# Where an expert's overflow blocks run in a one-core mixture-of-experts layer on Trainium2

## The reference, cut to what matters

```
top_logit, top_e = lax.top_k(logits, 4);  top_w = softmax(top_logit)
for every expert e, on the tokens routed to it:
    gu   = xb @ w_gu[e] + b_gu[e]                # 1024 -> 2048
    gate = min(gu[:, :1024], 7);  up = clip(gu[:, 1024:], -7, 7)
    act  = gate * sigmoid(1.702 * gate) * (up + 1)
    y    = act @ w_dn[e] + b_dn[e]               # 1024 -> 1024
    out[token] += y * w
```

## Time and profile before

| | |
|---|---|
| median of 3 runs | 1241.69 us (1239.27 to 1242.06) |
| the profiled execution's own time | 1241.96 us |
| its span on the core | 1240.2 us |
| TensorE matmuls busy | 1101.1 us, 89% |
| TensorE weight loads busy | 474.5 us, 38% |
| VectorE busy | 266.9 us, 22% |
| ScalarE busy | 146.2 us, 12% |
| GpSimd busy | 30.1 us, 2% |
| moved by DMA | 426.32 MB, mean 344 GB/s |
| SP's queue | 84.8% of 16 engines' span |
| mean granted TensorE clock | 0.966 |

### The profile page before, as it was taken

One profiled execution on the slowest core, in us unless ns is written; L12 is line 12 of the kernel. 1 busy time (PEld: TensorE's weight loads), 2 busy tenths in 40 slices (PEclk: granted clock), 3 DMA queues, 4 the chain that ended last, 5 costly groups with the idle time before them and its releaser, 6 DMA issues.

```text
span 1240.2 us, 14598 instructions
## 1 busy us (share of the span) xinstructions
PE 1101.1 (89%) x5388; PEld 474.5 (38%) x5389; DVE 266.9 (22%) x767; ACT 146.2 (12%) x309; POOL 30.1 (2%) x53
## 2 busy tenths in 40 slices
PE   7999796998899998989898878999989898989883
PEld 6677445333234332323232332433333232323221
DVE  2354535111112111121111111111211111111113
ACT  2144311100001000001000001001000010100000
POOL 3000410000000000000000000000000000000000
PEclk9999896998899999999999998999999999999997
DMA  9400849730999999999999958999999999999993
GB/s 314 181 1 1 262 191 393 294 137 17 419 419 418 419 418 418 418 417 417 418 419 418 418 232 326 418 417 418 417 418 418 418 418 418 419 418 418 417 414 120
DMA packets 80435, 426.32 MB, mean 344 GB/s; under 512 B 6025, under 2 KB 7610, under 8 KB 47610
## 3 DMA queue, kind: packets, MB, share of 16 engines
q1 hardware_dynamic: 79834, 425.37, 84.8%
q10 hardware_dynamic: 576, 0.61, 0.2%
HBM read 424.91 MB, written 1.05 MB: 343 GB/s over the span
## 4 chain that ended last, share of the span: by engine, by line
PE 50%; DMA 29%; SPq 14%; DVE 3%; issue 2%; ACT 1%; POOL 0%; DVEq 0%; POOLq 0%; ACTq 0%
PE PB L716 48%; DMA WB<-in_w_gate_up_dram 22%; SPq L331 6%; DMA WB<-in_w_down_dram 6%; SPq L326 6%; PE PB L1048 0%; DMA X<-in_x_dram 0%; SPq L335 0%; DVE S L1395 0%; PE PB L723 0%; DVE S L1524 0%; POOL K L478 0%; DVE WB L1289 0%; PE PB L806 0%; DVE S L1504 0%
## 5 line engine op out<-in xcount | busy, mean ns | idle before, releaser
L716 PE MATMUL PB<-WB,S 128*64 128x512 f32 (+5 forms) x3472 | 775.0, 596 | 72.3 <-DMA WB<-in_w_gate_up_dram 62.6
L716 PEld LDWEIGHTS PB<-WB,S 128*64 128x64 f32 (+2 forms) x3472 | 250.0, 140 | 562.8 <-issue 410.5
L1498 DVE TENSOR_SCALAR S<-PB 128x512 f32<-128x512 f32 (+1 forms) x34 | 23.5, 692 | 604.8 <-PE PB L716 604.8
L716 PE MATMUL PB<-S 32*64 32x512 f32 (+5 forms) x464 | 113.7, 594 | 4.9 <-issue 2.5
L659 ACT ACTIVATE S<-S 128x512 f32<-128x512 f32 x32 | 20.2, 630 | 556.4 <-DVE S L1498 556.4
L716 PE MATMUL PB<-S,X 128*128 128x128 f32 (+1 forms) x576 | 75.7, 293 | 9.3 <-DVE S L1524 8.0
L716 PEld LDWEIGHTS PB<-S,X 128*128 128x128 f32 x576 | 72.4, 208 | 23.7 <-issue 21.9
L716 PEld LDWEIGHTS PB<-S 32*64 32x64 f32 (+4 forms) x464 | 41.6, 164 | 65.0 <-issue 58.0
L1542 DVE COPY S<-PB 64x512 f32<-64x512 f32 x32 | 21.9, 683 | 205.4 <-PE PB L716 205.4
L716 PE MATMUL PB<-S,WB 128*128 128x256 f32 (+2 forms) x336 | 63.7, 391 | 0.4 <-ACT S L498 0.4
L716 PEld LDWEIGHTS PB<-S,WB 128*128 128x128 f32 (+1 forms) x336 | 49.5, 178 | 12.5 <-issue 2.1
(11 more groups left out here) (199 smaller groups left out, 339.4 us busy)
## 6 DMA issues: line engine op xcount, KB each, us to landing
WB<-in_w_gate_up_dram SPq DMA_DIRECT2D x128, 2048.0 KB, 22.8
WB<-in_w_down_dram SPq DMA_DIRECT2D x128, 1024.0 KB, 23.0
WB<-in_w_in_dram SPq DMA_DIRECT2D x1, 3088.0 KB, 15.2
WB<-in_w_in_dram SPq DMA_DIRECT2D x1, 3072.0 KB, 20.3
WB<-in_w_in_dram SPq DMA_DIRECT2D x1, 2144.0 KB, 11.1
WB<-in_w_in_dram SPq DMA_DIRECT2D x1, 2048.0 KB, 16.1
WB<-in_w_out_dram SPq DMA_DIRECT2D x2, 1024.0 KB, 10.2
WB<-in_w_out_dram SPq DMA_DIRECT2D x1, 2048.0 KB, 16.7
```

The lines of the kernel that those rows point to most:

```text
L716: return mm_(o, l, r, start=start, stop=stop, skip_group_check=True)
L1498: ts(g, gate, LIMIT, None, ALU.min).then_inc(s[g_ok], 1)
```

## The change

Each expert's extra blocks run at the end of its own gate-up's step, in front of the next expert's gate-up, instead of behind its down. For odd E they now stand right behind the transposes of E's activations in part 1 of the loop, and for even E behind `combine` in part 2. Expert 0's stand ahead of the loop; the number of calls stays 32, of which one is ahead of the loop, 30 are in it and one is behind it (before: none, 30 and two). Since the expert's down has not run yet, the extra block's down waits for each chunk of the down weights itself. The extra gather goes into bank 4 instead of 6; the extra gate-up waits until bank 6 has been copied out (`actT` or `ct_sb`); the wait for the down output copies stands before the transposes, not before the gather. VectorE makes the next expert's bias rows (`next_expert_rows`) ahead of the output copy instead of behind it. SP's program is not changed.

```diff
@@ scalar: extra_slots, and the order
-                act.activation(yx[:, 0:KT * XSLOTS], PB[6][:, 0:KT * XSLOTS], ACT.Copy).then_inc(s["xxg"], 1)
+                act.activation(yx[:, 0:KT * XSLOTS], PB[4][:, 0:KT * XSLOTS], ACT.Copy).then_inc(s["xxg"], 1)
...
             combine_weights(1)
+            extra_blocks(0)
             with act.Fori(0, PAIRS - 1) as i:
                 sigmoid(2 * i + 2)
                 slots_to_sbuf(0, 6, 2 * i + 3)
                 slots_to_sbuf(1, 4, 2 * i + 4)
                 expert_output(0, 2 * i + 1)
-                extra_blocks(2 * i)
                 act_columns(6, 2 * i + 2)
+                extra_blocks(2 * i + 1)
                 sigmoid(2 * i + 3)
                 expert_output(1, 2 * i + 2)
-                extra_blocks(2 * i + 1)
                 act_columns(5, 2 * i + 3)
                 combine_weights(i + 2)
+                extra_blocks(2 * i + 2)
             sigmoid(N_EXPERTS)
             expert_output(0, N_EXPERTS - 1)
-            extra_blocks(N_EXPERTS - 2)
             act_columns(6, N_EXPERTS)
+            extra_blocks(N_EXPERTS - 1)
             expert_output(1, N_EXPERTS)
-            extra_blocks(N_EXPERTS - 1)
@@ tensor: the extra block
-            def extra_gather(outputs_copied):
+            def extra_gather():
...
-                pe.wait_ge(s["ysb_ok"], outputs_copied + 1)
-                pe.wait_ge(s["ysb_dv"], outputs_copied)
                 pe.wait_ge(s["xoh"], xc)
...
-                        ins = mm(PB[6][:, XSLOTS * k:XSLOTS * k + XSLOTS], x_sb[:, b, P * k:P * k + P], ohx[:, b, :],
+                        ins = mm(PB[4][:, XSLOTS * k:XSLOTS * k + XSLOTS], x_sb[:, b, P * k:P * k + P], ohx[:, b, :],
...
-            def extra_blocks(e, t, n):
+            def extra_blocks(e, loaded, t, pb6_copied, copies, outputs_copied):
...
-                        extra_gather(n)
+                        extra_gather()
+                        pe.wait_ge(s[pb6_copied], copies)
                         for c in range(GU_CHUNKS):
                             extra_gate_up_chunk(c, e).then_inc(s["xguc"], 1)
                         extra_gate_up_bias(e).then_inc(s["xgu"], 1)
+
+                        pe.wait_ge(s["ysb_ok"], outputs_copied + 1)
+                        if not (isinstance(outputs_copied, int) and outputs_copied == 0):
+                            pe.wait_ge(s["ysb_dv"], outputs_copied)
                         extra_act_transposes()
...
                         for c in range(DN_CHUNKS):
+                            pe.wait_ge(s_dnl[e][c], 16 * loaded)
                             extra_down_chunk(c).then_inc(s["xdnc"], 1)
@@ tensor: the order
             combine()
+            extra_blocks(0, 1, 0, "ct_sb", 1, 0)
...
                 pe.wait_ge(s["xg_ok"], 2 * i + 4)
-                extra_blocks(0, 2 * i, 2 * i + 1)
                 act_transposes(6, 2 * i + 2)
+                extra_blocks(1, i + 1, 2 * i + 1, "actT", 2 * i + 2, 2 * i + 1)

                 gate_up(0, i + 2, 2 * i + 3)
                 down(1, i + 1, 2 * i + 2)
-                extra_blocks(1, 2 * i + 1, 2 * i + 2)
                 act_transposes(5, 2 * i + 3)
                 weight_transposes()
...
                 combine()
+                extra_blocks(0, i + 2, 2 * i + 2, "ct_sb", i + 2, 2 * i + 2)
...
             down(0, PAIRS, N_EXPERTS - 1)
-            extra_blocks(0, N_EXPERTS - 2, N_EXPERTS - 1)
             act_transposes(6, N_EXPERTS)
+            extra_blocks(1, PAIRS, N_EXPERTS - 1, "actT", N_EXPERTS, N_EXPERTS - 1)
             down(1, PAIRS, N_EXPERTS)
-            extra_blocks(1, N_EXPERTS - 1, N_EXPERTS)
@@ vector: the order in the loop (ahead of and behind it as on the other engines)
                 expert_activations(2 * i + 2)
+                next_expert_rows(0, 2 * i + 1)
                 expert_output(0, 2 * i + 1)
-                extra_blocks(2 * i, 2 * i + 2)
-                next_expert_rows(0, 2 * i + 1)
+                extra_blocks(2 * i + 1, 2 * i + 2)
                 expert_activations(2 * i + 3)
+                next_expert_rows(1, 2 * i + 2)
                 expert_output(1, 2 * i + 2)
-                extra_blocks(2 * i + 1, 2 * i + 3)
-                next_expert_rows(1, 2 * i + 2)
+                extra_blocks(2 * i + 2, 2 * i + 3)
                 next_one_hots(i + 1)
```

More of the change, by code:

```diff
@@ L1568, in _ @@
             expert_activations(1)
+            extra_blocks(0, 1)
             next_one_hots(0)
@@ L1581, in _ @@
             expert_output(0, N_EXPERTS - 1)
-            extra_blocks(N_EXPERTS - 2, N_EXPERTS)
+            extra_blocks(N_EXPERTS - 1, N_EXPERTS)
             expert_output(1, N_EXPERTS)
-            extra_blocks(N_EXPERTS - 1, N_EXPERTS)
             dve.wait_ge(s["comb"], PAIRS + 1)
```

## The result

The changed kernel takes 1225.22 us in the median of 4 runs (1222.96 to 1227.19), against 1240.48 us for the kernel before on the same chip: a ratio of 0.9876, with a 95% interval of 0.9852 to 0.9901. So it is faster by 12 to 20 us, 1.0% to 1.6%; the forecast was 1223.7 us.

What follows compares the result with a forecast made beforehand. Weight DMA was taken as the limit, so only its pauses could shrink: 11.4 (gap 2) + 4.8 (gap 1) + 1.8 (tail) = 18.0 us off 1241.96 gives 1224.0, forecast 1223.7 us; 8-in-10 range 1219 to 1229.

Steps and rivals of the forecast that it cites:

- What bounds the kernel: Weight loads at 418 GB/s set the time and TensorE follows; the change gains only from the DMA's pauses.
- Gap 2: DMA pause of 20.5 us from 730.5 us, around expert 15's extra block; the change was to gain 11.4 us.
- Gap 1: DMA pause of 32.3 us from 276.5 us, around expert 1's extra block; the change was to gain 4.8 us.
- The two skips: First jumps over unused extra-block bodies, ahead of the loop and at its end: 0.5 and 2.5 us, together taken as 2.7.
- a body jumped over for the first time: Reading of the earlier trace's single 4.98 us branch, median 208 ns: the price of a body's first skip.
- The wait for down weights: The extra block's down, now ahead of the expert's own, waits for its weights: 0 us, bounds 0 and 1.
- Bank 4 and the moved waits: Extra gather in another bank, copy waits and bias rows moved: cost 0, or 0.6 us without the one-hots' cover.
- Tail: Last skipped call no longer between the last down and combine: 1.8 us gained, bounds 0 and 1.8.
- More: Rival: the extra block runs at full clock in its new place, up to 3 us shorter; 1218 to 1220 us, chance 0.08.
- Less: Rival: each skipped body pays the first one's price, TensorE losing 2.5 us a pair; 1228 to 1230 us, chance 0.07.
- no change: Rival: something else keeps the two gaps; 1241.7 us, chance 0.05.
- slower: Rival: pause moves to E+1's down load and TensorE runs at 1.2 GHz from the gather; about 1259 us, chance 0.05.

Runs made afterwards that it cites:

- after_again: The changed kernel unaltered, measured again in a second, longer series: 1223.59 us against 1242.49 us for the kernel before, ratio 0.9859.
- after_no1: The changed kernel with expert 1's extra-block count set to 0, expert 15's block kept: 1197.36 us.
- before_no1: The kernel before with expert 1's extra-block count set to 0, expert 15's block kept: 1206.6 us.
- before_notail: The kernel before without the last extra-blocks call, expert 31's, between the last down and combine: 1238.69 us, ratio 0.9981.
- after_warm: The changed kernel with five matmuls, results unread, ahead of each extra block's wait for its one-hots: 1219.95 us, ratio 0.9837.
- down_first: The changed kernel, but an odd expert with an extra block runs its own down right behind it, ahead of the next gate-up: 1235.9 us.
- before_none: The kernel before with the counts of all extra blocks set to 0: 1185.41 us.

## Why the prediction was right, and where its terms were off

**What bounds the kernel**: right. The counts set to 0 give back 54.3 us by the spans, the pauses are 52.8, and no pause is left.

**Gap 2**, predicted 11.4 us, measured 7.9 by the chunk waits (7.4 in after_again) and 9.5 in the profiles without expert 1's block. The steps held in kind: no pause behind the gather, then one at E+1's down load. The mis-sized term is the block's length: I took its 29.0 us from the earlier trace rows, and it was 30.9. The window from 705 to 712 us shows a granted clock of 0.50, the gather took 7.04 us and the extra gate-up 9.63, where the kernel before had 6.79 and 8.64:

```profile
745.61 8.64 PE L716 MATMUL PB<-WB,S 128*32 128x512 f32 x64 [0.47 <-ACT S L638]
```

That made the pause 11.0 instead of 8.9 us. In after_no1 the same block, with the same wait in front of it, lasted 708.30 - 679.12 = 29.2 us, near the 29.0, and the pause there, from 717.7 to 727.1 us, is 9.4:

```profile
679.12 6.49 PE L716 MATMUL PB<-S,X 128*128 128x32 f32 x32 [3.41 <-DVE S L1528]
...
708.30 13.95 PE L716 MATMUL PB<-WB,S 128*64 128x512 f32 x64
```

```profile
715.00:720.00 5.00, 5.00 (x26) 1.64 (x24) 0.00 (x0) 0.00 (x0) 0.00 (x0) 1.00 0.55 228
...
725.00:730.00 5.00, 5.00 (x26) 1.55 (x22) 1.36 (x4) 0.00 (x0) 0.00 (x0) 1.00 0.67 240
```

So the pause follows the block's length as worked out. In both pairs the pause shrank by some 1.6 us more (9.5, and 11.1 from before_no1's 20.5) than the chunk waits behind it show (7.9 and 9.5); these 1.6 us I can't place.

**Gap 1**, predicted 4.8 = 7.5 - 2.7, measured 5.1 by the chunk waits, and up to 7.8 with before_notail's profile for the kernel before. The two skips cost less than the 2.7: the one ahead of the loop stalled TensorE 1.39 us, where 0.5 was predicted (branch 5.94 us instead of 4.98), and the one at the loop's end cost nothing (branch 353 ns) instead of 2.5. (The second sum was also off: 325.1 + 1.1 + 4.98 is 331.2 and not 331.4, so 2.3.) Without the skips the 7.5 of the prediction stand against 5.1 + 1.4 = 6.5 in this pair of profiles and against 6 to 10 by subtraction of the medians. That 4.8 and 5.1 are so near is luck in part: the skips were 1.3 us too dear in the sum and the rest 1.0 too large.

**The reading of the earlier trace rows**, "a body jumped over for the first time", was wrong. A first skip can also cost nothing. These are two of the changed kernel:

```profile
L1106 PEldq COMPARE_BRANCH  x1: 5936/5936/5936, 235.9 to 235.9; - x1
...
L1106 PEldq COMPARE_BRANCH  x1: 353/353/353, 325.6 to 325.6; - x1
```

The skip over expert 31's body took 344 ns there (342 in after_again) and 6320 ns in after_warm, where this body is ten matmul instructions longer. In down_first the body and its call are unedited, only the loop in front of them is longer, and it took 6972 ns:

```profile
L1106 PEldq COMPARE_BRANCH  x1: 6972/6972/6972, 1196.7 to 1196.7; - x1
```

So with other code ahead of it an unedited call stalled. That fits the rule cited in the prediction from the Trainium skill (Runtime: NRT & Kernel Launch, Instruction fetch mechanics), which speaks of the target's place and not of the first time; which part of the code the sequencer held was not tried. Nor is it shown that the place alone decides. TensorE's code is the same in before_none and before_no1, and the same first skip took 5.40 us in one and 0.83 in the other:

```profile
L1109 PEldq COMPARE_BRANCH  x1: 5395/5395/5395, 263.0 to 263.0; - x1
```

```profile
L1109 PEldq COMPARE_BRANCH  x1: 827/827/827, 263.2 to 263.2; - x1
```

What decides the length of a stall stays open.

**The wait for down weights**: right, none. The time to spare in gap 1 was misread: the DMA stops at 276.5 us, and the block reaches its down at 272.5 + 318.81 - 296.93 = 294.4, so it is 18 us and not 14; nothing hangs on it. **Bank 4 and the moved waits**: right, no wait of theirs shows. **Tail**: predicted 1.8; the stall gave 1.7, and 1.7 more came from a combine at the full clock, which I had not counted. The run alone says 2.4 (0.9 to 4.0).

**Sum**: 18.0 predicted, 16.9 in the profiles and 15 to 19 in the medians. Gap 2 came out 3.5 us too high and the tail 1.6 too low, so the sum is better than its parts: that much of the hit is luck.

**The rivals.** "More" did not happen: the 4 us of idle in front of the gather stayed and the clock fell in it, as its counter-argument said (0.57 and 0.50 over the two gathers). Its price was sized right (3 us a block; 3.0 and 4.3 with TensorE kept busy). "Less", "no change" and "slower" did not happen; the pause did move to E+1's down load, but at 11 us and not longer. The 35 us in "slower" do not follow from its own terms: 14 us of gate-up and about as much of block in each of two gaps is 56, which would have given some 1280 us. Its condition did not occur: the clock is 1.00 in the gate-up behind either block (the windows from 300 and from 743 us).

## What to carry to other kernels

Where one queue issues all loads in order, look for the pause and ask which buffer's release it waits for; after the fix ask again, since the next release in the order is late next. Here it was TensorE itself, so a few us of idle in front of its first matmul of a block cost twice, once as wait (3.4 to 3.7 us) and about once more as slow matmuls (3.0 and 4.3), and making an operand earlier on VectorE gave nearly as much as moving the block. Moving work up can also uncover what it had hidden, as the early down did.

## What the runs showed that I had not expected

In thirteen profiles the branch over a skipped extra block took 207 to 427 ns on TensorE's sequencer or 5.0 to 7.0 us, for the same source line and the same outcome; in between lie 0.83 and 1.46 us in before_no1 and 1.82 us in before_none. (Where the body is entered it is 77 to 96 ns.) Five matmuls whose results nothing reads made each block 3.0 to 4.3 us shorter: the granted clock was 1.00 over the gather and not 0.57 or 0.50. And the same unedited code, from the kernel's start to the router, put the first load behind it at 219.64 to 223.07 us in the thirteen profiles, which is more than some of the effects looked for here: such an offset has to be taken out before two spans are compared. Even then one execution can mislead by 2 to 3 us, as before_notail shows.
